# TensorE's four expert turns: a loop of one written turn, against four turns written one after the other

## The reference, cut to what matters

```python
hm = x * (1 + sc2) + sh2
# grouped_moe: the best group by the sum of its top-2 affinities, then the top-2 experts in it
for e in range(N_EXPERTS):                      # 16 experts, 2048 -> 1024 -> 2048
    hid = jax.nn.silu(t @ w_gate[e]) * (t @ w_up[e])
    y = y + combine[:, e:e + 1] * (hid @ w_down[e])
x = layer_norm(DEEPNORM_ALPHA * x + g2 * f, ln2_g[l], ln2_b[l])
```

## Time and profile before

| | us |
|---|---|
| median of 3 runs | 1911.14 (1908.58 to 1911.75) |
| the profiled execution, its own time | 1910.54 |
| its span, first to last instruction | 1908.7 |
| TensorE busy | 1749.4 (92%) |
| VectorE busy | 508.8 (27%) |
| ScalarE busy | 163.5 (9%) |
| moved by DMA | 629.77 MB, mean 330 GB/s |

### The profile page before, as it was taken

How to read it: one execution, slowest core, us unless ns; L and a number is a source line. 1 busy time by engine, 2 the same in 40 slices (tenths; PEclk the granted TensorE clock), 3 DMA queues, 4 the chain that set the end, 5 groups by cost and what they waited for, 6 DMA issues and landing times.

```text
span 1908.7 us, 21648 instructions
## 1 busy us (share of the span) xinstructions
PE 1749.4 (92%) x8982; PEld 957.5 (50%) x8983; DVE 508.8 (27%) x944; ACT 163.5 (9%) x342; POOL 2.5 (0%) x9
## 2 busy tenths in 40 slices
PE   6889999999999999979999879999889888899984
PEld 4337888688888884454433224332243222433321
DVE  1441536656364101150031120211111111112114
ACT  0001013100000000032000002000020000200000
POOL 0000000000000000000000000000000000000000
PEclk9889999999999999989999999999999999999997
DMA  9995975678677634432789996999999999799995
GB/s 384 425 393 158 374 325 209 265 297 339 268 307 311 269 125 198 167 143 80 280 352 429 429 425 275 395 428 428 428 389 429 428 428 428 300 406 410 427 427 219
DMA packets 51000, 629.77 MB, mean 330 GB/s; under 512 B 5775, under 2 KB 8240, under 8 KB 11848
## 3 DMA queue, kind: packets, MB, share of 16 engines
q1 hardware_dynamic: 49768, 623.15, 78.7%
q10 hardware_dynamic: 1120, 5.00, 0.7%
HBM read 624.46 MB, written 3.67 MB: 329 GB/s over the span
## 4 chain that ended last, share of the span: by engine, by line
PE 76%; DMA 17%; DVE 3%; issue 2%; SPq 1%; ACT 0%; ACTq 0%; DVEq 0%
PE bank L959 42%; PE bank L689 20%; PE bank L701 9%; DMA ring<-in_w_down 8%; DMA ring<-in_w_up_gate 8%; PE bank L713 3%; DMA ring<-in_w_in 1%; DVE ada_rows L1582 1%; PE bank L708 1%; SPq L471 1%; PE bank L755 1%; PE bank L991 1%; SPq L464 0%; DVE region_a L1541 0%; DVE region_a L1532 0%
## 5 line engine op out<-in xcount | busy, mean ns | idle before, releaser
L689 PE MATMUL bank<-ring,region_b 128*64 128x512 f32 x1792 | 402.7, 597 | 31.7 <-DMA ring<-in_w_up_gate 23.2
L959 PE MATMUL bank<-region_a,ring 128*128 128x256 f32 x1792 | 390.3, 380 | 0.0
L959 PEld LDWEIGHTS bank<-region_a,ring 128*128 128x128 f32 x1792 | 340.3, 190 | 48.6 <-issue 3.8
L689 PEld LDWEIGHTS bank<-ring,region_b 128*64 128x64 f32 x1792 | 123.8, 137 | 284.5 <-issue 245.1
L701 PE MATMUL bank<-ring,region_f 128*64 128x512 f32 (+1 forms) x1408 | 233.4, 519 | 21.9 <-DMA ring<-in_w_down 21.9
L1582 DVE SCALAR_TENSOR_TENSOR ada_rows<-ring,condT,ada_rows 128x512 f32<-128x512 f32 x293 | 220.2, 752 | 10.0 <-DMA ring<-in_ada_w 0.2
L701 PEld LDWEIGHTS bank<-ring,region_f 128*64 128x64 f32 (+1 forms) x1408 | 76.8, 127 | 161.8 <-issue 127.2
L1903 DVE TENSOR_TENSOR region_a<-bank,region_a 128x512 f32<-128x512 f32 x128 | 79.5, 683 | 220.3 <-PE bank L713 220.3
L959 PE MATMUL bank<-ring,region_b 128*128 128x512 f32 x256 | 110.3, 593 | 1.3 <-issue 1.3
L959 PE MATMUL bank<-ring,region_a 128*128 128x512 f32 x160 | 76.9, 635 | 6.2 <-DMA ring<-in_w_in 5.4
L959 PE MATMUL bank<-region_e,region_x 128*128 128x256 f32 x256 | 65.2, 422 | 18.2 <-issue 15.2
(11 more groups left out here) (180 smaller groups left out, 858.4 us busy)
## 6 DMA issues: line engine op xcount, KB each, us to landing
ring<-in_w_up_gate SPq DMA_DIRECT2D x112, 2048.0 KB, 21.8
ring<-in_w_down SPq DMA_DIRECT2D x56, 2048.0 KB, 22.8
ring<-in_ada_w SPq DMA_DIRECT2D x44, 2048.0 KB, 11.7
ring<-in_w_in SPq DMA_DIRECT2D x31, 2048.0 KB, 16.2
region_g<-in_w_up_gate SPq DMA_DIRECT2D x16, 2048.0 KB, 22.8
ring<-in_w_branch SPq DMA_DIRECT2D x8, 2048.0 KB, 17.7
ring<-in_w_out SPq DMA_DIRECT2D x8, 2048.0 KB, 11.2
region_g<-in_w_down SPq DMA_DIRECT2D x8, 2048.0 KB, 23.9
```

What stands on the lines that cost most here:

```text
L689: last = nc.tensor.matmul(bank_of(x, j)[n * c:n * c + n, 0:2 * m], tokens(x, 8 * half + k), w[:, k % 4, :, m * c:m * c + m], start=(half = ...
L959: return nc.tensor.matmul(out, lhsT, rhs, start=start, stop=stop)
```

## The change

The loop is gone. Python runs over g = 0 to 3 and writes the turn's instructions four times, so g is a number and not a register. With it go the register of the turn number, its increment, the closing branch and its hint. Each turn has its own hint mark for the jump to the long body (`large_announced[g]`), its own labels (`pe{g}_{le}`), and its own copies of the long bodies, which all stand behind the stage. The alignment to slot 104 stays ahead of the first turn alone.

```diff
-            turn_no = nc.alloc_registers("expert_turn", engines=kinds)
-            nc.regs_mov(turn_no, 0)
             pe.addr_align(bass.FETCH_BLOCK_INSTRUCTIONS, offset=LOOP_SLOT, max_nops=0)
-            nc.br("pe_expert_turn", engines=kinds)
-            with nc.body("pe_expert_turn", valid_engines=kinds):
-                g = nc.snap(turn_no, min_val=0, max_val=NE // GRP - 1)
-                large_announced = pe.mark_branch_hint_location()
-                pe.wait_ge(hot_ready, g + 1)
...
+            nc.br("pe_experts", engines=kinds)
+            with nc.body("pe_experts", valid_engines=kinds):
                 asked = []
-                for le in range(GRP):
-                    if le == 1:
-                        back_announced = pe.mark_branch_hint_location()
-                    count = pe.value_load(counts[0:1, bass.ds(expert_at(g, le), 1)], min_val=0, max_val=T)
-                    here = few_tokens(pe, f"pe{le}", count, lambda xs: expert_pe(pe, mm, g, le, xs),
-                                      large_announced if le == 0 else None)
-                    asked.append((count, here))
-                nc.regs_alu(turn_no, turn_no, 1, op=mybir.AluOpType.add)
-                pe.br_lt(turn_no, NE // GRP, on_true="pe_expert_turn", on_false="pe_experts_end").branch_hint(back_announced)
+                for g in range(NE // GRP):
+                    large_announced[g] = pe.mark_branch_hint_location()
+                    pe.wait_ge(hot_ready, g + 1)
...
+                    for le in range(GRP):
+                        e = expert_at(g, le)
+                        count = pe.value_load(counts[0:1, e:e + 1], min_val=0, max_val=T)
+                        here = few_tokens(pe, f"pe{g}_{le}", count, lambda xs: expert_pe(pe, mm, g, le, xs),
+                                          large_announced[g] if le == 0 else None)
+                        asked.append((g, le, count, here))
+                nc.br("pe_experts_end", engines=kinds)
             nc.switch_bb("pe_experts_end")
-            for le, (count, here) in enumerate(asked):
-                more_tokens(pe, f"pe{le}", mybir.EngineType.PE, count, here, lambda xs: expert_pe(pe, mm, g, le, xs))
+            for g, le, count, here in asked:
+                more_tokens(pe, f"pe{g}_{le}", mybir.EngineType.PE, count, here,
+                            lambda xs: expert_pe(pe, mm, g, le, xs))
```

## The result

The kernel with the turns written out takes 1889.25 us (median of 4 runs, 1888.28 to 1890.39) against 1910.1 us (4 runs) of the kernel before: a ratio of 0.9891 with a 95% interval of 0.9874 to 0.9908, 20.9 us less. The forecast was 1894 us, with a range of 1889 to 1905 us, so the result lies inside the range by 0.25 us, at its fast end. The profiled execution took 1888.28 us, with a span of 1886.5 us.

The account below looks back on a forecast made before the run. DMA was taken to bound most of the expert stage, TensorE the turn heads. Savings of 6.85, 3.7 (capped) and 6.65 us, together 17.2 us, took 1910.54 to 1893.3 us, median 1894 us; range 1889 to 1905 us.

Parts of the forecast that it names:

- The missed code fetch: Between last scatter and next gather: closing branch's target is absent; 0.5 us stays, 4.0, 4.75 and 5.0 us saved.
- The clock: In the three gathers: half clock behind the gap loses 2.85, 2.35 and 1.65 us, counted as saved.
- the dip at the extra gather of turn 1: Extra gather, 3.39 us against 1.93 us in turn 3: cause stays, nothing counted, 1.46 us as upper bound.
- The pauses as cap: At turn heads TensorE's earlier arrival gains up to the DMA pause: 10.9, 3.7 and 13.3 us in turns 1 to 3.
- What was counted at nothing: Register arithmetic ahead of TensorE's waits: nothing, bound 1.02 us once; long-body jumps: zero, turn 0 moving up to 3.11 us.
- the first rival: Some long-body jumps miss: two to four at 2.7 us, 5 to 11 us back, 1899 to 1905 us; chance 0.25.
- third: All six long-body jumps miss at the full gap of 5.48 us: slower, about 1927 us; chance 0.05.
- the same hints stand at the same distances: Reason for taking zero cost at the long-body jumps, with 2.7 us for each of two to four kept in the range.

Follow-up runs that it names:

- far jump: Written-out kernel with turns 2 and 3 behind the long bodies of turns 0 and 1, reached by an unhinted plain jump ending turn 1; 1890.98 us.
- the body of two turns: Against the written-out kernel: turns 0 and 1 written as one body, run twice, one closing branch left between turns 1 and 2; 1903.63 us.
- its later hint: Kernel before the change, with the closing branch's hint given at the fourth expert of the turn in place of the second; 1909.36 us, ratio 0.9997.
- the edge 2 to 3: Against the written-out kernel: turns 0 and 1 written out, turns 2 and 3 a loop, one closing branch left between them; 1900.09 us.
- the near loops: Written-out kernel plus, ahead of each turn, a loop of two rounds with one register addition and a compare-and-branch back to itself; 1892.72 us.
- the register: Written-out kernel with the turn number in a register again, for waits and the read of the counts, without the closing branch; 1891.76 us, ratio 0.9893.
- the repeated gather: Written-out kernel with the last two of eight gather pieces computed twice, in turn 2 (1888.46 us) or in turn 1 (1893.56 us).

## Why the prediction was right, and where it was short

**The missed code fetch.** Right, and now shown from four sides: the gap goes when the code is in order, comes back at a loop's edge, comes back at a plain far jump, and does not come for a near branch. The instruction packets go with it: one in each gap, none where there is no gap. The residue is 0.1 us, not the 0.5 us that was taken: 0.4 us too little for each turn. What was called a hinted edge that "finds its target absent" holds for the loop of one turn; the body of two turns shows that a hinted edge can hit, and the kernel without hints that a jump without a hint can too.

**The clock.** Right in kind. The three gathers gained 2.59, 2.12 and 1.44 us, where 2.85, 2.35 and 1.65 us were counted (the full-clock gather is 14.05 us, not 13.8 us). For the dip at the extra gather of turn 1 nothing was counted, and 3.39 us became 1.92 us, 1.47 us more. This is not the change's doing. The kernel before with its later hint kept all three gaps and had 1.92 us there, while four kernels without that gap had 3.33 to 3.84 us (the one with the edge 2 to 3, the one with two turns as one body, the one with the near loops, the one with the register). The dip comes and goes, and the two traces compared happened to have it and not.

**The pauses as cap.** The rule held: where the DMA queue pauses, what makes TensorE earlier is gained up to the length of the pause. Turn 2 gained 3.55 us of the 7.3 us that TensorE saved, where 3.7 us were forecast; turn 3 gained 6.55 us against 6.65 us. The far jump and the repeated gather show the cap directly. The pause of turn 1 was read too short: behind the 12 us at a share of 0.09 stand 10 us at 0.49 (1170 to 1180 us), 5 us more, and 0.85 over the first 120 us is 18 us in all. The cap did not bind there, so nothing in the sum hung on it. Turn 1 gained 9.23 us against 6.85 us: 4.4 us of gap, 2.6 us of gather and 1.5 us of extra gather are 8.5 us of it; 0.3 us is the shorter hop ahead of the extra gather (0.75 to 0.47 us); 0.4 us is not assigned.

**What was counted at nothing.** Turn 0 was 1.5 us shorter, of which 0.47 and 0.37 us are the issue waits around its long body (3.11 to 2.64, 1.02 to 0.65 us). The front up to the first gather, whose code is the same, was 1.37 us shorter. That is chance: over the kernels run here the first gather started anywhere from 851.03 to 852.88 us. Turn 0 of the changed kernel itself was 279.26 us once and 275.67 us another time. Between them lies the clock: from 870 to 890 us it was 0.83 in the first and 1.00 in the second. Of these 3.6 us, 2.3 us came back in turn 1, in a stretch that waits for weights (34.90 and 37.28 us between the same two scatters).

In sum the term that came out larger is turn 1, by 2.4 us; with turn 0 and the front it makes the 5 us between 17.2 us and the 22.3 us of the two profiled executions (1910.54 and 1888.28 us). But two executions of one kernel share the time differently between turns 0 and 1. In the second one turn 1 gained 6.95 us, as forecast, and turn 0 gained 5.1 us, where nothing was forecast. Turns 0 and 1 together gained 10.7 and 12.0 us against 6.85 us, and that is the part of the sum that was short. Of the 5 us, the dip (1.5 us) and the front (1.4 us) are chance. That the number lies in the range is luck: it is inside by 0.25 us, less than the executions differ, and the second set of runs, 1888.37 us, would lie outside. The three terms of the gap, the gather and the cap are right without it.

**The rivals.** The first and third could have come true. The kernel with two turns as one body paid for two missed long-body jumps, 5.5 and 7.6 us of turn, where the first rival took 2.7 us each. About 2 us of each are a slow extra gather (3.84 and 4.24 us in place of 1.92 us); the rest is still more than 2.7 us, as a miss on the way back had no eviction to hide behind and the clock was down after it. The kernel without hints paid for five. That the written-out layout spares them was a matter of where the code happens to lie, and the argument "the same hints stand at the same distances" was weaker than I made it. What decides between hit and miss stays open: it is not the time of the hint alone (no effect in the kernel before), and the length of the body or its place changed it. No run varied the place alone, for which another `LOOP_SLOT` would have been enough.

## What to carry to other kernels

A gap of several us put down to "issue" at a loop's edge or a far jump, with an instruction packet in it, and none at like places without a gap, was a fetch in this kernel; price it by the same view at other jumps, and add what the clock loses behind it. Then ask what TensorE's lateness delays. Where the DMA queue pauses because all places are full, taking a delay away gains time up to the length of that pause and not beyond. Adding one costs in full where a pause stands already (turn 1), and where none stands the first part is free, about 4 us in turn 2. Before a difference is given to a change, have a second execution of both kernels: single turns moved by up to 3.6 us here with no change. And after any change of code layout look at all far jumps anew, since a miss can move from one to another.

## What had not been expected

A hinted closing branch of a body of two turns cost nothing, while the same edge of a body of one turn cost 4.3 to 5.5 us, and the misses turned up at the jump back from the long body of its second copy (4.26 and 5.20 us) instead. A jump without a hint, the one back in turn 3, cost nothing. TensorE's waits on semaphores worked out from a register were longer by up to 0.28 us (0.75 to 0.47 us ahead of the extra gather), but this did not lengthen a turn.
